# MLP up products of a two-block model: high weights times both parts of the rows in one product of 512 columns

## The reference

```python
def conv_mlp(h, w_up, conv_w, w_down):      # h: (1, 256, 1024), w_up: (1024, 2 * 2816)
    u = dwconv3(h @ w_up, conv_w)            # u_t = w0*p_(t-1) + w1*p_t + w2*p_(t+1), per channel
    gate, val = u[..., :2816], u[..., 2816:]
    return (jax.nn.silu(gate) * val) @ w_down
```

## Time and profile before

| | us |
|---|---|
| timed runs, median of 3 | 684.61 (683.48 to 685.54) |
| profiled execution, time | 682.7 |
| profiled execution, span from the first to the last instruction | 680.7 |
| TensorE busy | 637.0 |
| VectorE busy | 379.1 |
| ScalarE busy | 277.7 |

### The profile page before, as it was taken

How to read it: one execution, slowest core, us unless ns; L and a number is a source line. 1 busy time by engine, 2 the same in 40 slices (tenths; PEclk the granted TensorE clock), 3 DMA queues, 4 the chain that set the end, 5 groups by cost and what they waited for, 6 DMA issues and landing times.

```text
span 680.7 us, 11095 instructions
## 1 busy us (share of the span) xinstructions
PE 637.0 (94%) x4347; PEld 482.7 (71%) x4347; DVE 379.1 (56%) x666; ACT 277.7 (41%) x431; POOL 56.1 (8%) x81
## 2 busy tenths in 40 slices
PE   7999999999999999999999999999999987668895
PEld 4999997799999999996598788744444432315364
DVE  5696965768766666666769456352222221203195
ACT  6763373656555555545774831220111110000193
POOL 1000000400000000002074620000000000000010
PEclk9999999999999999999999999999999998898998
DMA  9943542747655555302933448899899999999931
GB/s 323 328 172 126 194 141 67 267 149 243 235 186 185 185 185 186 128 0 101 392 142 123 139 172 320 350 430 428 354 430 430 425 425 428 428 428 427 405 128 62
DMA packets 55208, 174.75 MB, mean 257 GB/s; under 512 B 4742, under 2 KB 29442, under 8 KB 48898
## 3 DMA queue, kind: packets, MB, share of 16 engines
q1 hardware_dynamic: 54496, 172.54, 66.2%
q10 hardware_dynamic: 674, 1.69, 0.7%
HBM read 173.17 MB, written 1.05 MB: 256 GB/s over the span
## 4 chain that ended last, share of the span: by engine, by line
PE 73%; DMA 14%; DVE 7%; ACT 2%; issue 2%; another core or an unknown queue 0%; POOL 0%; POOLq 0%; DVEq 0%; ACTq 0%
PE ps L1809 15%; PE ps L1811 15%; PE ps L1810 15%; DMA W<-in_w_moe_dram 7%; DMA spare<-in_w_moe_dram 6%; PE ps L2326 6%; PE ps L2310 3%; PE ps L2386 3%; PE ps L2332 2%; PE ps L2006 2%; PE ps L1781 1%; PE ps L2433 1%; PE ps L2154 1%; DVE arena L1466 1%; PE ps L2105 1%
## 5 line engine op out<-in xcount | busy, mean ns | idle before, releaser
L1809 PE MATMUL ps<-hT_high,w_up_parts 128*128 128x256 f32 x352 | 99.9, 284 | 0.0
L1811 PE MATMUL ps<-hT_high,w_up_parts 128*128 128x256 f32 x352 | 99.7, 283 | 0.0
L1810 PE MATMUL ps<-hT_low,w_up_parts 128*128 128x256 f32 x352 | 99.7, 283 | 0.0
L1809 PEld LDWEIGHTS ps<-hT_high,w_up_parts 128*128 128x128 f32 x352 | 67.6, 192 | 0.5
L1810 PEld LDWEIGHTS ps<-hT_low,w_up_parts 128*128 128x128 f32 x352 | 67.6, 192 | 0.4
L1811 PEld LDWEIGHTS ps<-hT_high,w_up_parts 128*128 128x128 f32 x352 | 67.6, 192 | 0.0
L1297 DVE TENSOR_TENSOR w_up_parts<-W,w_up_parts 128x1024 fp32r<-128x1024 f32 x44 | 53.2, 1235 | 24.3 <-ACT w_up_parts L826 24.3
L826 ACT CAST w_up_parts<-W 128x1024 fp32r<-128x1024 f32 x44 | 44.7, 1047 | 28.5 <-PE ps L1811 28.5
L2326 PE MATMUL ps<-W,junk 128*32 128x512 f32 x368 | 46.2, 630 | 7.5 <-DMA W<-in_w_moe_dram 7.5
L996 ACT ACTIVATE sg<-ps 128x256 f32<-128x256 f32 x9 | 3.5, 384 | 121.4 <-PE ps L2326 121.4
L1809 PE MATMUL ps<-h_high,dense_high 128*128 128x256 f32 x160 | 45.8, 286 | 0.0
(11 more groups left out here) (480 smaller groups left out, 1318.7 us busy)
## 6 DMA issues: line engine op xcount, KB each, us to landing
W<-in_w_moe_dram SPq DMA_DIRECT2D x22, 2048.0 KB, 21.1
arena<-in_w_moe_dram SPq DMA_DIRECT2D x14, 2048.0 KB, 30.0
W<-in_w_up_dram SPq DMA_DIRECT2D x22, 1024.0 KB, 8.8
W<-in_w_in_dram SPq DMA_DIRECT2D x8, 2048.0 KB, 10.9
W<-in_w_down_dram SPq DMA_DIRECT2D x11, 1024.0 KB, 5.1
spare<-in_w_moe_dram SPq DMA_DIRECT2D x5, 2048.0 KB, 20.7
hh<-in_w_moe_dram SPq DMA_DIRECT2D x4, 2048.0 KB, 32.7
W<-in_w_out_dram SPq DMA_DIRECT2D x2, 2048.0 KB, 9.3
```

The costliest lines, as they stand in the source:

```text
L1809: pe.matmul(o, lhs[0], rhs[0], start=first, stop=False, skip_group_check=True)
L1810: pe.matmul(o, lhs[0], rhs[1], start=False, stop=False, skip_group_check=True)
L1811: return pe.matmul(o, lhs[1], rhs[0], start=False, stop=last_k, skip_group_check=True)
```

## The change

For the high weights the two products (rows high, rows low) become one of 512 columns. Its moving operand takes both parts of the rows for one k, and its output fills a whole bank: columns 0 to 255 take high x high, columns 256 to 511 high x low. The low weights times the high rows are added, as a product of 256 columns, to the first half. So a chunk has a bank of its own (bank c), used by every pair, and the two halves have to be added: ScalarE copies the second half to the buffer `us` in `spare` (`copy_low`), VectorE adds the first half to it in place (`add_low`). All taps then read `us` in SBUF. TensorE waits per chunk for `us_ready` of the same chunk a pair earlier. To make room for the new semaphores `ub_ready` and `us_ready`, `par_done` and `params_out` join shared ones.

```diff
@@ hT
-        hT_hl = [v3(t, KD) for t in split_pair("hT", W_at, 0, 2048)]
+        hT_both = rounded("hT_parts", W_at, 0, 4096).rearrange("p (part k t) -> p part k t", part=2, k=KD)
+        hT_hl = [hT_both[:, part] for part in range(2)]
+        us = v3(spare[:, 0:1024], 4)
@@ ScalarE
+            def copy_low(p, c):
+                act.wait_ge(sig("up_used"), p * 4 + c + 1)
+                if not (isinstance(p, int) and p == 0):
+                    act.wait_ge(sig("tap_done"), p * 8 + 1)
+                act.copy(us[:, c, :], ps[:, c, SEQ:2 * SEQ]).then_inc(sig("ub_ready"), 1)
+
             def conv_mlp(p, q, h, more=True):
-                if more:
-                    split_up(p + 1, 1 - q, h + q)
-                act.wait_ge(sig("up_used"), p * 4 + 4)
+                for c in range(4):
+                    copy_low(p, c)
+                    if more:
+                        split_up(p + 1, 1 - q, h + q, (c,))
+                act.wait_ge(sig("us_ready"), p * 4 + 4)
                 act.wait_ge(sig("cw_ready"), p + 1)
...
-                        act.activation(c[:, i, :], ps[:, 2 * q + i, 256 * g:256 * g + 256], ACT.Copy,
+                        act.activation(c[:, i, :], us[:, 2 * i + g, :], ACT.Copy,
                                        scale=w).then_inc(sig("centre_done"), 1)
@@ ScalarE, last pair
                 act.copy(last_dn[0][i], DN[0][:, i]).then_inc(sig("down_high"), 1)
-                act.wait_ge(sig("up_used"), p * 4 + 2 * i + 2)
+                for c in (2 * i, 2 * i + 1):
+                    copy_low(p, c)
+                act.wait_ge(sig("us_ready"), p * 4 + 2 * i + 2)
@@ VectorE
+            def add_low(p, c):
+                dve.wait_ge(sig("ub_ready"), p * 4 + c + 1)
+                dve.tensor_tensor(us[:, c, :], ps[:, c, 0:SEQ], us[:, c, :], ALU.add).then_inc(sig("us_ready"), 1)
+
             def conv_mlp(p, q, h, more=True):
-                if more:
-                    split_up(p + 1, 1 - q)
+                for c in range(4):
+                    add_low(p, c)
+                    if more:
+                        split_up(p + 1, 1 - q, (c,))
...
-                            u = ps[:, 2 * q + i, 256 * g:256 * g + 256]
+                            u = us[:, 2 * i + g, :]
@@ TensorE
             def up(p, q):
-                if not (isinstance(p, int) and p == 0):
-                    pe.wait_ge(sig("tap_done"), p * 8 - 7)
                 for c in range(4):
+                    if not (isinstance(p, int) and p == 0):
+                        pe.wait_ge(sig("us_ready"), p * 4 + c - 3)
                     pe.wait_ge(sig("up_low"), p * 4 + c + 1)
-                    i, g = divmod(c, 2)
-                    o = ps[:, 2 * q + i, 256 * g:256 * g + 256]
                     for k in range(KD):
...
-                        last = product(o, [t[:, c, k, :] for t in w_up_hl], [t[:, k, :] for t in hT_hl], k == 0, k == KD - 1)
+                        pe.matmul(ps[:, c, :], w_up_hl[0][:, c, k, :], hT_both[:, :, k, :], start=(k == 0), stop=False,
+                                  skip_group_check=True)
+                        last = pe.matmul(ps[:, c, 0:SEQ], w_up_hl[1][:, c, k, :], hT_hl[0][:, k, :], start=False, stop=(k == KD - 1),
+                                         skip_group_check=True)
```

More of the change, by code:

```diff
@@ L76, in build @@
         STEPS = {
-            "pe_mix1": (("lr_done", 1), ("q_done", 1), ("pre_done", 2), ("k_done", 1), ("v_done", 2), ("gc_done", 2),
+            "pe_mix1": (("par_done", 1), ("lr_done", 1), ("q_done", 1), ("pre_done", 2), ("k_done", 1), ("v_done", 2), ("gc_done", 2),
                         ("scores_done", 4), ("kot_done", 2), ("gv_done", 2), ("kv_done", 3), ("gb_done", 2),
@@ L91, in build @@
                          ("skip_ready", 4), ("e_ready", 6), ("pT_ready", 1)),
-            "dve_mix1": (("z_ready", 2), ("rest_half", 1), ("cum_ready", 1), ("qk_ready", 6), ("PT_ready", 4),
+            "dve_mix1": (("params_out", 3), ("z_ready", 2), ("rest_half", 1), ("cum_ready", 1), ("qk_ready", 6), ("PT_ready", 4),
                          ("m_ready", 2), ("conv_a", 9), ("ya_ready", 1), ("oms_ready", 1), ("on_ready", 2),
@@ L873, in _ @@
                 act.copy(last_dn[0][i], DN[0][:, i]).then_inc(sig("down_high"), 1)
-                act.wait_ge(sig("up_used"), p * 4 + 2 * i + 2)
+                for c in (2 * i, 2 * i + 1):
+                    copy_low(p, c)
+                act.wait_ge(sig("us_ready"), p * 4 + 2 * i + 2)
                 for g, c in ((0, cgt[0]), (1, cvt[0])):
                     w = cwp[0][:, 6 * g + 3 * i + 1:6 * g + 3 * i + 2]
-                    act.activation(c[:, i, :], ps[:, i, 256 * g:256 * g + 256], ACT.Copy, scale=w).then_inc(sig("centre_done"), 1)
+                    act.activation(c[:, i, :], us[:, 2 * i + g, :], ACT.Copy, scale=w).then_inc(sig("centre_done"), 1)
                 act.wait_ge(sig("tap_done"), p * 8 + 5 + 4 * i)
@@ L1099, in _ @@
             normed(0)
-            dve.wait_ge(sig("par_done"), 1)
+            dve.wait_ge(sig("par_done"), at("par_done", 1))
             link(dve.tensor_copy(par[:, 0:NROW], ps[:, 7, 0:NROW]))
@@ L1334, in conv_mlp @@
                    .then_inc(sig("uact_low"), 1)
-            dve.wait_ge(sig("params_out"), 3)
+            dve.wait_ge(sig("params_out"), at("params_out", 3))
             dve.sem_inc(sig("tap_done"), 1)
@@ L1356, in _ @@
                         w = cwp[0][:, 6 * g + 3 * i + 2 * side:6 * g + 3 * i + 2 * side + 1]
-                        u = ps[:, i, 256 * g:256 * g + 256]
+                        u = us[:, 2 * i + g, :]
                         if side == 0:
@@ L1829, in _ @@
             pe.wait_ge(sig("hT_ready"), 4)
-            pe.wait_ge(sig("params_out"), 3)
+            pe.wait_ge(sig("params_out"), at("params_out", 3))
             pe.wait_ge(sig("wlr_landed"), 16)
```

## The result

| | before | changed |
|---|---|---|
| timed runs on one chip, median us | 685.01 (683.48 to 685.82, 6) | 687.62 (687.03 to 689.74, 6) |
| ratio | 1 | 1.0044 (95% interval 1.0027 to 1.0062) |
| profiled execution, time / span | 682.7 / 680.7 | 687.0 / 685.0 |

The changed kernel is slower by 2.6 us. Its 687.62 lies inside the range of the prediction (682.4 to 688.4), but outside the likeliest case's own range (684.3 to 686.4), which said no change that can be told. It is over the 686.66 from which the prediction called the kernel slower, with a chance of 0.26.

The account below looks back on a forecast made before the run. TensorE's instruction stream was taken to bound the MLP loop. up(2) to up(9) save 3.10 us, the last tile costs 3.84, so +0.74 on the median of 684.61 gives 685.3 us; range 682.4 to 688.4.

Parts of the forecast that it names:

- the likeliest case: Whole program: 685.3 us, within 0.3% and so no change that can be told, 684.3 to 686.4; chance 0.54.
- two slow rivals: MLP: VectorE sets the loop's pace (688.9 us, chance 0.18), or the mixed stream saves nothing (688.4 us, chance 0.10).
- The bound: MLP loop: only TensorE's instruction stream counts, busy for all of a 16.98 us period, VectorE for 11.86.
- What TensorE saves: Up products: two of 256 columns become one of 512, saving 0.0121 us each, 0.39 us a pair of tiles.
- The 0.24 to 0.2175: Up products: bounds for one 512-column product, from no gain (0.240 us) to the bf16 row's rate (0.2175 us).
- the rule of the Trainium skill: Up products: N/2.4 + 2.5 ns per isolated warm matmul, so 0.64 us saved over up(2) to up(9), estimate 687.8.
- The first tile: MLP's start: down(0) still starts at about 152.98; the 0.77 us saved by up(0) and up(1) become idle time.
- VectorE in the loop: MLP loop: VectorE's own period grows from 14.47 to 15.93 us, against TensorE's new 16.59, so it still catches up.
- the loop falls to VectorE: MLP loop: VectorE's period passes 16.2 us; at 16.6 it sets the pace throughout, 688.9 us; chance 0.18.
- What the last tile pays: Last tile's chain: adds and waiting centre taps cost 1.70 us a half; last uact_low +3.84 against up(9)'s end.
- Behind the last tile: After the MLP: later stages and loads move with its end, no added cost; TensorE's earlier idle stretch about 4 us.
- gains nothing or nearly so: Up products: the mixed stream saves nothing, leaving only the last tile's cost, +3.8, 688.4 us; chance 0.10.

Follow-up runs that it names:

- Experiments 1: Model left out, only streams of products: 512 and 256 columns in turn, parts apart or together; 0.3533 us a k-step together, 512-column product alone 0.2267.
- experiment 3: Changed kernel with high and low parts of the rows side by side for each k; 687.62 us, ratio 1.0035.
- experiment 5: Model left out, product streams told apart by line; 96 k-steps each: in turn 0.3533 us, eight and eight 0.3490, two of 384 columns 0.3467.
- experiment 2: Changed kernel with the last pair as before the change (three products of 256 columns, taps from PSUM, no copy or add); 682.03 us, ratio 0.9958.
- experiment 4: Changed kernel with 13 unread bf16 filler products in TensorE's wait for the last uact_low; 686.8 us, ratio 1.0022.
- experiment 10: experiment 2 measured once more, unchanged, on another occasion; 682.89 us, ratio 0.9983.
- the grouped kernel: experiment 2 with each chunk's eight products of 512 columns first, then its eight of 256; 683.02 us, ratio 0.9981.

## Why the prediction was partly right

The time fell into the range because the range took in two slow rivals; the sum itself forecast +0.7 and +2.6 was measured. One term of the sum was mis-sized and one was missing, and both made the kernel slower than forecast.

**The bound.** Right. In the loop only TensorE's stream counts; every stretch of the difference is read on it.

**What TensorE saves: the step that was mis-sized.** "I take 0.0121, since its row has the same type and the same number of columns." The row was that of a stream of equal products. In turn with 256 columns a k-step takes (187.67 - 176.38)/32 = 0.3528, where 0.2279 + 0.1200 = 0.3479 was counted, so 0.3600 - 0.3528 = 0.0072 is saved in place of 0.0121 (the mark of no gain was 0.36). The 0.24 to 0.2175 that bounded the cost of the long product held it: 0.3528 - 0.1200 = 0.2328. For eight pairs that is 8 x 32 x 0.0072 = 1.8 us in place of 3.10, and the table shows 1.54 for the stretch: the 24 down products of a turn take 176.38 - 170.87 = 5.51 us where they took 5.47, which takes some 0.3 off again. Experiments 1, 3 and 5 put the loss on the change of length. By the rule of the Trainium skill that the prediction weighed against its own ("TensorE: Matmul & The Clock Gate", "Back-to-back issue gap"), 2.5 ns a pair of products, it would be 0.64 us there. The trace agrees with neither: 1.54 lies between 0.64 and 3.10.

**The first tile.** Nearly right. TensorE's idle time ahead of down(0) is 1.19 us, below the 1.3 to 1.5 expected. up(0) and up(1) end 0.42 us sooner, not 0.77 (their last product starts 152.55 - 129.87 = 22.68 us behind the first, against 152.17 - 129.07 = 23.10). The chain to `uact_low` is 1.19 - 0.53 - 0.42 = 0.24 us later than "at about 152.98", counted from the first up product.

**VectorE in the loop.** Right, to 0.02 us. Its timeline behind TensorE, which answers to the earlier trace rows; L1321 is `add_low`:

```profile
153.18 0.69 DVE L1353 TENSOR_TENSOR uact_low<-arena,uact_high 128x512 fp32r<-128x512 f32 x1 [0.75 <-ACT uact_high L868]
153.79 0.42 DVE L1321 TENSOR_TENSOR spare<-ps,spare 128x256 f32<-128x256 f32 x1
...
169.09 0.69 DVE L1353 TENSOR_TENSOR uact_low<-arena,uact_high 128x512 fp32r<-128x512 f32 x1 [0.76 <-ACT uact_high L868]
```

Its period is 169.09 - 153.18 = 15.91 against 15.93 forecast, below TensorE's 16.80. The rival "the loop falls to VectorE" did not happen: no idle time of TensorE between 154.01 and 312.24. The add was well priced from its nearest row (0.42), and so were the taps from SBUF: 480 ns, against 477 from PSUM in the profile before

```profile
L1342 DVE SCALAR_TENSOR_TENSOR arena<-spare,arena 128x255 f32<-128x255 f32 x80 | 33.4, 480 | 18.6 <-ACT arena L857 18.3
```

**What the last tile pays.** Right, +3.62 for +3.84. VectorE's timeline with one row of ScalarE, against the earlier trace rows:

```profile
302.21 1.23 DVE L1372 TENSOR_TENSOR w_up_parts<-W,w_up_parts 128x1024 fp32r<-128x1024 f32 x1 [1.19 <-ACT w_up_parts L884]
303.35 0.75 DVE L1321 TENSOR_TENSOR spare<-ps,spare 128x256 f32<-128x256 f32 x2
...
305.08 1.80 DVE L1384 SCALAR_TENSOR_TENSOR arena<-spare,arena 128x255 f32<-128x255 f32 x4 [0.98 <-ACT arena L890]
...
309.28 1.23 DVE L1372 TENSOR_TENSOR w_up_parts<-W,w_up_parts 128x1024 fp32r<-128x1024 f32 x1 [0.45 <-ACT w_up_parts L884]
...
315.45 0.43 DVE L1390 TENSOR_TENSOR uact_low<-arena,uact_high 128x256 fp32r<-128x256 f32 x1 [0.54 <-ACT uact_high L894]
```

```profile
304.13 0.91 ACT L890 ACTIVATE arena<-spare,arena 128x256 f32<-128x256 f32 x2 [1.49 <-DVE spare L1321]
```

Split, two adds, centre taps at 304.13, side taps at 305.08: 2.87 us behind the split in place of 1.14, so 1.73 where 1.70 was counted. From split to split a half takes 7.07 us against 5.33 in experiment 2. Only the start of the chain moved less than counted (302.21 - 288.43 = 13.78 against 13.63 before, +0.15 for +0.44).

**Behind the last tile: the step that was missing.** "Behind it the mixture, the norm and the expert stage start from the MLP's end". They do, and the loads move along as said: the long piece of the earlier trace rows starts at 546.37 in place of 541.79. But the idle stretch "of about 4 us" was priced only as time waited. It also took the clock: +1.58 us in the trace; in the medians some 0.8, within the noise of these runs. The stretch itself was in the prediction, and the kernel before already keeps its clock with filler products in other waits (`keep_busy`); to ask what an idle stretch does to the work behind it would have found the term.

**The sum.** With the measured saving the forecast's own terms give 0.74 + 1.56 = +2.3 against the kernel before, which is near the +2.6 of the timed runs; with the clock's 1.58 they give +3.9, which is the +3.89 of the traces. The rival "gains nothing or nearly so" had the direction right and, with +3.8, its size by the traces, but not its reason: half of the saving was lost, not all, and the rest was the clock's.

## What to carry to other kernels

Price a new stream of instructions by its pattern, not by the sum of the rates of its parts, and when a saving is 3% of a step, measure the step. A longer chain behind the last tile is paid in full, and here, where TensorE stood idle for 3.7 us in front of it, again by the clock in the trace; take the last tile out of such a change (experiment 2: from 2.6 us slower to 1.4 to 2.9 faster). One trace beside one trace can differ by 0.8 us at one place that nobody edited, and by 1.2 to 2.9 us at another; compare them stretch by stretch, with the granted clock beside each.

## What the hardware showed that was not expected

- Products of 512 and 256 columns in turn take 0.3533 us, in groups of eight 0.3490, two of 384 columns 0.3467, all for 768 columns at full clock (experiment 5).
- Behind 3.69 us of idle time the granted clock stayed at 1.00 for the first half microsecond of work (0.3 us in experiment 3), was then 0.50 for more than 3 us of dense products, and came back. Behind 0.89 us of idle time (experiment 4) it stayed at 1.00.
- The same place of the same kernel runs at a granted clock of 1.00 in one execution and near 0.50 in another: ahead of the MLP (0.7 us) and between 362 and 374 us (1.2 us in experiment 10 and not in experiment 2).
- The trace of the grouped kernel is 1.55 us shorter in the MLP and its median over 12 executions is not shorter. What a profile gives for a gain of this size still has to be seen in the timed runs.
